# Twelve matmuls of a weight unit, reordered into four triples that share a stationary tile, in a two-layer decoder trunk

## What is computed

```python
def reference(x, ...):
    for l in range(DEPTH):                                  # DEPTH = 2
        h = _rmsnorm(x, attn_norm[l])
        x = x + _hybrid_mixer(h, lam_init, w_in[l], ...)    # h @ w_in, three attentions, branches, @ w_out
        h = _rmsnorm(x, ffn_norm[l])
        gate, up = jnp.split(h @ w_gate_up[l], 2, axis=-1)
        x = x + (jax.nn.silu(gate) * up) @ w_down[l]
    return x
```

## Time and profile before

| | |
|---|---|
| median of 3 runs | 2871.65 us (2871.58 to 2873.06) |
| profiled execution, first to last instruction | 2869.4 us |
| PE busy | 2863.4 us, 100% |
| weight loads (PEld) busy | 2372.1 us, 83% |
| DVE, ACT, POOL busy | 1852.1, 1339.4, 868.4 us |
| DMA | 567.39 MB, mean 198 GB/s |

### The profile page before, as it was taken

The page is one execution under the profiler, slowest core; times in us unless marked ns, Lnnn a source line. Parts: engine busy times, 40 slices in busy tenths (PEclk is TensorE's granted clock), DMA queues, the critical chain, the costliest instruction groups (busy, mean ns, idle before and its releaser), DMA issues.

```text
span 2869.4 us, 35463 instructions
## 1 busy us (share of the span) xinstructions
PE 2863.4 (100%) x12860; PEld 2372.1 (83%) x12860; DVE 1852.1 (65%) x2277; ACT 1339.4 (47%) x1564; POOL 868.4 (30%) x1477
## 2 busy tenths in 40 slices
PE   9999999999999999999999999999999999999999
PEld 8888888888888888888888888888888888888887
DVE  7599866687655555545575998666876555555554
ACT  5445554554544444444444455445545444444443
POOL 0055267355222322300000652773452313213000
PEclk9999999999999999999999999999999999999999
DMA  7666666776666666666666666667766666666554
GB/s 247 182 186 199 201 192 194 229 238 194 196 192 192 195 191 193 194 193 194 193 193 177 198 192 197 191 194 233 238 194 196 191 193 193 191 195 191 194 193 170
DMA packets 291296, 567.39 MB, mean 198 GB/s; under 512 B 18984, under 2 KB 24944, under 8 KB 291184
## 3 DMA queue, kind: packets, MB, share of 16 engines
q1 hardware_dynamic: 283888, 540.54, 61.8%
q10 hardware_dynamic: 7296, 25.44, 2.7%
HBM read 551.23 MB, written 14.68 MB: 197 GB/s over the span
## 4 chain that ended last, share of the span: by engine, by line
PE 98%; DVE 1%; ACT 0%; issue 0%; DMA 0%; DVEq 0%; ACTq 0%
PE acc L481 64%; PE acc L486 32%; PE acc L528 1%; DVE w_lo L1193 1%; PE acc L526 1%; PE acc L539 0%; DVE arena L1193 0%; DVE tmp L1193 0%; PE acc L519 0%; ACT w_hi L812 0%; PE acc L540 0%; DMA xs<-in_x_dram 0%; DVE arena L1211 0%; PE acc L498 0%; PE acc L654 0%
## 5 line engine op out<-in xcount | busy, mean ns | idle before, releaser
L1193 DVE TENSOR_TENSOR w_lo<-w_raw,w_hi 128x1024 fp32r<-128x1024 f32 x1024 | 1261.6, 1236 | 970.4 <-ACT w_hi L812 965.8
L812 ACT ACTIVATE w_hi<-w_raw 128x1024 fp32r<-128x1024 f32 x1024 | 1084.0, 1060 | 1461.4 <-PE acc L486 1414.6
L481 PE MATMUL acc<-w_hi,opa_hi 128*128 128x512 f32 (+1 forms) x2364 | 927.8, 392 | 0.6 <-ACT w_hi L812 0.6
L481 PE MATMUL acc<-w_hi,opa_lo 128*128 128x512 f32 (+1 forms) x2364 | 917.6, 388 | 0.0
L481 PE MATMUL acc<-w_hi,opb_hi 128*128 128x512 f32 x1728 | 672.9, 389 | 0.2
L481 PE MATMUL acc<-w_hi,opb_lo 128*128 128x512 f32 x1728 | 672.3, 389 | 0.0
L486 PE MATMUL acc<-w_lo,opa_hi 128*128 128x512 f32 (+1 forms) x2364 | 629.9, 388 | 0.1
L481 PEld LDWEIGHTS acc<-w_hi,opa_hi 128*128 128x128 f32 x2364 | 444.0, 188 | 94.4 <-issue 3.7
L486 PEld LDWEIGHTS acc<-w_lo,opa_hi 128*128 128x128 f32 x2364 | 442.7, 188 | 92.4 <-DVE w_lo L1193 2.0
L481 PEld LDWEIGHTS acc<-w_hi,opa_lo 128*128 128x128 f32 x2364 | 444.0, 188 | 88.2
L391 POOL COPY arena<-tmp 32x256 f32<-32x256 f32 x384 | 262.5, 684 | 732.3 <-DVE tmp L1211 717.3
(11 more groups left out here) (182 smaller groups left out, 1141.6 us busy)
## 6 DMA issues: line engine op xcount, KB each, us to landing
w_raw<-in_w_gate_up_dram SPq DMA_DIRECT2D x352, 512.0 KB, 4.4
w_raw<-in_w_in_dram SPq DMA_DIRECT2D x336, 512.0 KB, 3.6
w_raw<-in_w_down_dram SPq DMA_DIRECT2D x176, 512.0 KB, 4.6
w_raw<-in_w_branch_dram SPq DMA_DIRECT2D x64, 512.0 KB, 4.7
w_raw<-in_w_out_dram SPq DMA_DIRECT2D x64, 512.0 KB, 4.4
gate_store<-nat ACTq DMA_DIRECT2D x24, 512.0 KB, 3.9
arena<-gate_store ACTq DMA_DIRECT2D x24, 512.0 KB, 5.4
w_raw<-in_w_kv_b_dram SPq DMA_DIRECT2D x16, 512.0 KB, 4.3
```

The lines of the kernel that those rows point to most:

```text
L481: pe.matmul(bank(pair, t, width), op[j][:, kt + k, t * P:(t + 1) * P], w_hi[:, s, k, 0:width], start=(first and k == 0 and j == 0), stop=F ...
L812: return act.activation(out, in_, ACT.Copy, scale=scale)
L1193: return dve.tensor_tensor(out, a, b, op)
```

## The change

Within a unit the three matmuls of one k tile and one row tile now stand together: lo operand with `w_hi`, hi operand with `w_hi`, hi operand with `w_lo`. The second and the third have the same stationary tile. The wait for `lo_ready` stands ahead of the third matmul of the unit.

```diff
                 pe.wait_ge(hi_ready, n + (m + 1))
                 for k in range(KU):
                     for t in range(NT):
-                        for j in range(2):
-                            pe.matmul(bank(pair, t, width), op[j][:, kt + k, t * P:(t + 1) * P], w_hi[:, s, k, 0:width],
-                                      start=(first and k == 0 and j == 0), stop=False)
-                pe.wait_ge(lo_ready, lo_count(n, m))
-                for k in range(KU):
-                    for t in range(NT):
-                        mm = pe.matmul(bank(pair, t, width), op[0][:, kt + k, t * P:(t + 1) * P], w_lo[:, s, k, 0:width],
-                                       start=False, stop=(last and k == KU - 1))
+                        hi_op, lo_op = (op[j][:, kt + k, t * P:(t + 1) * P] for j in range(2))
+                        pe.matmul(bank(pair, t, width), lo_op, w_hi[:, s, k, 0:width], start=(first and k == 0), stop=False)
+                        pe.matmul(bank(pair, t, width), hi_op, w_hi[:, s, k, 0:width], start=False, stop=False)
+                        if (k, t) == (0, 0):
+                            pe.wait_ge(lo_ready, lo_count(n, m))
+                        mm = pe.matmul(bank(pair, t, width), hi_op, w_lo[:, s, k, 0:width], start=False,
+                                       stop=(last and k == KU - 1))
                 mm.then_inc(unit_done, 1)
```

## The result

The changed kernel takes 2877.58 us (median; 2877.41 to 2877.87) beside 2871.44 us for the kernel before in the same runs: ratio 1.0021, 95% interval 1.0013 to 1.0028. It is slower by 6.1 us, and the forecast was 2877.9. The span of the profiled execution is 2875.7 us, 6.3 more than before.

A forecast was written before the change was run, and what follows sets the result against it. TensorE bounds it: matmul count times spacing, plus PE's few waits. Delays of 3.50 + 1.36 + 1.36 = 6.2 us, set on the median 2871.65, give 2877.9 us; spread 2876 to 2880, with rivals 2874 to 2884.

The forecast's parts named there:

- The term taken as 0: Saving from the shared tile in 4092 pairs per kernel: at most 13.3 ns each, 54.4 us; the forecast took none.
- the repeated tile of the warm-up: Warm-up matmuls at L546, one stationary tile, 128 columns: 0.112 us apart, against 0.109 us for transposes with new tiles.
- The doubt that the prediction left there: A warm-up call has two passes whose loads may differ, so its tile might not truly repeat.
- The start: Start of layer 0: late `w_lo` in units 0, 3 and 5, chained through the transposes, cost 0.78 + 1.36 + 1.36 = 3.50 us.
- rival C: Start of layer 0: weights' arrival sets units 3 and 5, delays overlap to one of 1.36 us; total 2875.7 us; chance 0.14.
- The second part of the projections: Once per layer, PE waits for a late `w_lo` at unit 57, third matmul instead of ninth: +1.36 us each.
- Rival B: Second part of the projections: late units add up, near 4.2 us per layer instead of 1.36; total 2883.6 us; chance 0.12.
- Units 12 and 13: Near 45 us in layer 0: late by 0.3 to 0.4 us at most, covered by PE already 3.5 us behind: 0.
- the line that the prediction drew at 2877.4: Whole-kernel time above which a measurement can tell slower from no change, about 0.2% or 5.7 us.
- 13.3 ns beside the columns: Fixed part of every matmul's spacing, independent of width: 226.7 ns at 512 columns, of which the columns take 213.3.

## Why the prediction was right

**The spacing stays.** Predicted 226.7 ns at all three steps of a triple, measured 2649 matmuls in the same 600 us and steps of 0.23, 0.23 and 0.22 us; taking the 4092 pairs away moves the time by less than the scatter. The term taken as 0 rested on one thin row, the repeated tile of the warm-up. The doubt that the prediction left there (a call's two passes may load different halves) is settled by the unit of one tile.

The Trainium skill, page "TensorE: Matmul & The Clock Gate", section "Step-by-step: what each phase is for", has one load serve many matmuls. Here every matmul brings its own load, also behind the same tile, so no run shows a load that is saved. From the formula that the Trainium skill, page "TensorE: Matmul & The Clock Gate", section "Back-to-back issue gap", gives for an isolated gap, the estimate for 512 columns is 215.8 ns. That spacing appears in no run of this kernel, not even with one tile for a whole unit: there too it is 226.7, and the measurement decides.

**The start.** Predicted 0.78, 2.14 and 3.50 us after units 0, 3 and 5; read from the ends of the units 2.18 and 3.56 after units 3 and 5, of which 0.06 us lies ahead of unit 0; with unit 0 alone changed, its delay shows as 0.73. Apart from the rest the start costs 3.4 us. The step that mattered was to follow each delay to what PE's next instructions release: without the transposes the three places would have given one delay of 1.36, rival C.

**The second part of the projections.** Predicted 1.36 us per layer, read 1.37 and 1.42. The prediction placed the whole loss at unit 57, counted once; on PE it falls in units 54, 55 and 57, and the sum is the same, because the way over DVE has a fixed length and only its last release counts. Rival B, which added up the late units, asked for 4.2 us per layer.

**Units 12 and 13.** Predicted 0 because a late PE covers them. Right for the changed kernel, and the cover shows when it is taken away: 0.4 us, the top of the 0.3 to 0.4 that the prediction named.

**The chances.** 0.49 for slower, 0.39 for no change: the forecast lay 0.5 us beyond the line that the prediction drew at 2877.4, and the measurement lies 0.2 us beyond it (2877.58). The cost is well founded, since eight runs and the trace bear out its terms; that it fell on this side of so near a line is partly luck.

## What to carry to other kernels

In this kernel a wait that was moved earlier was free wherever its event came early, and was paid in full, steps moved times the time of a step, wherever the engine had met the event just in time. Such places were few and could be listed: look for the ends of the producer just ahead of the consumer, and follow each delay to what the late engine releases next, since only that tells whether two delays add or overlap. And before an order is changed so that an operand is used twice in a row, look whether the load goes away in the built program: here a repeated tile was loaded again each time, under a running matmul as before, and the spacing stayed at 226.7 ns.

## What was not expected of the hardware

The line through the widths 392 and 512, which leaves 13.3 ns beside the columns, was in the rows before. Not expected was how little moves the spacing: no two neighbours with the same tile, a pair in each triple, or one tile repeated eleven times give 2649 matmuls per 600 us each, to the last one. What the 13.3 ns are, no run here shows. It is not that the tile is a new one, since a load of the same tile leaves them as they are. Whether it is the load itself stays open: no kernel without the loads was tried.
